# VectorE turns three pairs of head blocks by 32x32 blocks, in place of TensorE transposes

## The chip, the cores and the metric

The kernel runs on one core of one Trainium2 chip. The metric is device time in microseconds (us), the median of a few executions. Names used below: PE is TensorE, PEld its weight loads, DVE is VectorE, ACT is ScalarE, POOL is GpSimd, SP is SyncE, which issues nearly all DMAs.

## The reference

Two layers of a float32 transformer over 256 tokens and a width of 1024. Each layer is a gated feed-forward block, a mixer of three attention branches, and a second feed-forward block. What matters here is the mixer's head work:

```
h = _rmsnorm(x, mix_norm[l])
a_q, a_kv, i_q, i_k, i_w, b_qkv, c_q, c_kv, c_g, m_g = jnp.split(h @ w_in[l], cuts, axis=-1)
i_q = _rope(i_q.reshape(B, T, IDX_HEADS, IDX_DIM), pos)            # 4 index heads of 64
i_k = _rope(i_k[:, :, None, :], pos)[:, :, 0]
y_a = _dsa_attention(a_q, a_k, a_v, i_q, i_k, i_w) @ w_branch_a[l]
b_qkv = b_qkv.reshape(B, T, 3, B_HEADS, HEAD_DIM)                  # 4 heads of 64
y_b = _moba_attention(_rope(b_qkv[:, :, 0], pos), _rope(b_qkv[:, :, 1], pos), b_qkv[:, :, 2]) @ w_branch_b[l]
```

The scores of every branch are products of queries and keys over the 64 columns of a head, and are multiplied by 64 ** -0.5 = 0.125 before the softmax (branches A, B and C; the index scores have a factor of their own).

## The kernel before

**Slabs.** All weights stream through three buffers, slab by slab of 128x2048 values (1 MB, two DMAs of 512 KB). A slab m goes through four hands. SP loads it into `raw` as soon as VectorE has finished slab m-3 (semaphore `lo_done`). ScalarE rounds it into `whi`, once TensorE is done with slab m-3 (`slab_used`). VectorE forms `wlo = raw - whi` (`convert`, L509). TensorE then does three matmuls for each product (L1311 to L1313): with `whi`, with `wlo`, and with the low part of the activations. A full slab is 24 matmuls of 512 columns.

**The projection stage of the mixer.** Slabs 0 to 9 of the mixer are five column groups u = 0 to 4 of `h @ w_in`, two slabs for each. Slabs 10, 11 and 12 are narrow (660, 660 and 440 columns), slab 13 and those behind it are gate weights. When TensorE has done a group, ScalarE copies it out to `proj` (`project_out`, L1153), and VectorE applies the rotation to the heads in it (`rope`, L637 to L643) and leaves the rotated heads in `rs`, which lies in the tile `gates`. `rs` has one block of 128 columns for each two heads: blocks 3 and 4 are the index queries, 6 and 7 branch B's queries, 8 and 9 its keys.

**The order on VectorE** is written out by hand in `mixer`: convert two slabs (m even, m odd), then `rope` of the group whose copy out has just been done, and so on. `rope(l, 1)` stands behind slab 5, `rope(l, 2)` behind slab 7, `rope(l, 3)` behind slab 9, `rope(l, 4)` behind slab 11. Every engine runs its own instructions strictly in that order.

**Fills.** Scores need the heads with the head's columns on partitions, so each block of `rs` is transposed. `FILLS` lists these: TensorE transposes one or two blocks into a PSUM bank (`fill`, L1481; a pair of blocks is four transposes of 128x128), and ScalarE or VectorE copies the bank into `q_t` or `k_t` (`copy_fill`), in turn by the fill's number: even ones ScalarE, odd ones VectorE. The first T1 = 5 fills stand on TensorE between slab 12 and slab 13, the others between slab 13 and slab 14. Fills marked "qs" are scaled by 0.125 on the way.

**Maxima.** For each pair of head groups VectorE adds a mask to the scores and takes row maxima in one operation (`maxima`, L708); the factor -1.0 in it turns the sign, and ScalarE takes the exponential with scale -1.0.

Of the kernel before, what the change touches and what calls it, by code (L numbers as in the profile page):

```python
# [33 lines left out]
P = 128  # L34
SEQ, D, DFF, DEPTH = 256, 1024, 2816, 2
NT = SEQ // P
# [45 lines left out]

FILLS = [((0, 1), "qs", 0), ((2,), "pair", 0), ((3, 4), "q", 2), ((6, 7), "qs", 4), ((8, 9), "k", 2),
         ((14,), "pair", 4), ((15,), "pair", 6), ((10, 11), "qs", 6), ((12, 13), "qs", 8),
         ((16, 17), "n", 0), ((18, 19), "n", 2)]
NFILL = len(FILLS) + 2
T1 = 5

# [23 lines left out]

LAST_ORDER = [0, 2, 1, 3]

V_STEPS = 246
SETUP_WARM, SETUP_G = 1, 19  # L120


def build(nc, x_in, ffn1_w_gate, ffn1_w_up, ffn1_w_down, w_in, cmp_w1_k, cmp_w2_k, cmp_w1_v, cmp_w2_v,
# [3 lines left out]
    with ctx:  # L127
# [229 lines left out]
        def prob_view(b, t):  # L357
            a, w = (0, P) if t == 0 else (512, SEQ)
            return prob[:, b, a:a + 4 * w].rearrange("p (h c) -> p h c", h=4)
# [129 lines left out]
        def _(dve):  # L489
# [156 lines left out]
            def fill_out(l, f):  # L646
# [2 lines left out]
                copy_fill(lambda o, i, k: step(nc.vector.tensor_scalar(o, i, k, None, ALU.mult)), f)  # L649
                at_step["fill", f] = count[0]  # L650

            def cmp_windows(l):

                dve.wait_ge(fill_a, l * 7 + 7)
                own(l)
                for v in range(2):
                    for g in range(2):
                        for a in range(2):
                            win = kvs[:, v, g, 16 * a:16 * a + CMP_STRIDE * NCMP]\
                                .rearrange("p (n j r) -> p j n r", j=8, r=2)[:, :, :, 0]  # L660
                            o = cmpm[:, v, 8 * a:8 * a + 8, g * CPAD:g * CPAD + NCMP]
                            pb = pos_c(l, v)[:, 8 * a:8 * a + 8].unsqueeze(2).broadcast_to([P, 8, NCMP])
                            step(nc.vector.tensor_tensor(o, win, pb, ALU.add), ("windows",))
# [34 lines left out]
            def maxima(l, e):  # L698
                pair, b = PAIRS[e], e % 2
                own(l)  # L700
                dve.wait_ge(sc_ps, l * len(PAIRS) + e + 1)
                if pair != "C":

                    masks = sel_b if pair == "A" else future_b
                    for t in range(NT):
                        mk = masks[:, 0:P] if t == 0 else masks[:, P:3 * P]
                        for h in range(4):
                            step(nc.vector.tensor_tensor_reduce(prob_view(b, t)[:, h, :], score_head(t, h), mk, -1.0,  # L708
                                                                -TAKEN, ALU.add, ALU.min,
                                                                nmax[:, b, 4 * t + h:4 * t + h + 1]), ("max", e, t))  # L710
                if pair == "C":
                    o = prob[:, b, 0:256].rearrange("p (h c) -> p h c", h=16)
                    for t in range(NT):
                        step(nc.vector.tensor_tensor(o[:, 8 * t:8 * t + 8], ps[:, 4, t * P:(t + 1) * P]
                                                     .rearrange("p (h c) -> p h c", h=8),
                                                     kmask_b[:, t, :].unsqueeze(1).broadcast_to([P, 8, CPAD]), ALU.add))
                    own(l)
                    step(nc.vector.tensor_reduce(nmax[:, b, :], o, AX_X, ALU.max, negate=True))
                    own(l)
                    step(nc.vector.tensor_tensor(o, o, nmax[:, b, :].unsqueeze(2).broadcast_to([P, 16, CPAD]),  # L720
                                                 ALU.add), ("max", e, 0))
# [107 lines left out]
            def mixer(l):  # L829
                S = FFN_SLABS  # L830
                prep(l, 1, (2, 3), [2, 3])
                step(nc.vector.memset(cmpm[:, :, :, :], 0.0), ("cmpm zero",))
                last_width = {S + m: nk * LASTU for m, _, nk in M_LAST}
                for m in range(2, 14):
                    convert(l, S + m, last_width.get(S + m, SLAB))
                    if m % 2 and m < 12:
                        rope(l, m // 2 - 1)
                for f in range(1, T1, 2):
                    fill_out(l, f)
                rope(l, 5)  # L840
                convert(l, S + 14)
                dve.wait_ge(cg_done, l + 1)
                step(nc.vector.tensor_scalar(cgt[:, :, :], cgt[:, :, :], 0.5, 0.5, ALU.mult, ALU.add))
                own(l)
                step(nc.vector.tensor_tensor(cgt3[:, :, :, 0], cgt3[:, :, :, 0],
                                             valid[:, :].unsqueeze(2).broadcast_to([P, NT, 8]), ALU.mult))
                for f in range(T1, NFILL, 2):
                    fill_out(l, f)
                cmp_windows(l)
                convert(l, S + 15)  # L850
                hidden_rows(l)
                convert(l, S + 16)
                hidden(l)
                index_scores(l, 0)
                compressed_out(l)
                convert(l, S + 17)
                rounds = [0, 0, 1, 1, 1, 1, 1, 3, 0, 0]
                done = 0
                for e in range(len(SLOTS)):
                    k, before = pair_at(e), pair_at(e - 1)  # L860
                    if e == 1:
                        index_scores(l, 1)
                    if e > 0 and k is not None:
                        maxima(l, k)
                    if e == 4:
                        heads_rest(l, 0)
                    if e == 6:
                        heads_rest(l, 1)


                    late = k in (1, len(PAIRS) - 1)
                    if e > 0 and not late:
                        convert(l, S + 17 + e)
                    if e > 0 and k is not None:
                        scaled(l, k, 0)
                    for _ in range(rounds[e]):
                        select_round(l, done)
                        done += 1
                    if k is not None and k > 1:
                        scaled(l, k, 1)  # L880
                    if late:
                        convert(l, S + 17 + e)
                assert done == 8
                heads_rest(l, 2)
                heads_rest(l, 3)
                convert(l, S + 27)
                for g in range(4):
                    gated(l, 1, g)
                convert(l, S + 28)
                gated(l, 0, 0)  # L890
                gated(l, 0, 1)
                convert(l, S + 29)
                gated(l, 2, 0)
                gated(l, 2, 1)
                gated(l, 0, 2)
                gated(l, 0, 3)
                turned_rest(l, 0)
                turned_rest(l, 1)
                gated(l, 2, 2)
                gated(l, 2, 3)  # L900
                convert(l, S + 30)
                convert(l, S + 31)
                for n in range(2, 4):
                    turned_rest(l, n)
                for m in range(32, 34):
                    convert(l, S + m)
                residual(l, 1, 0, 1.0, S + 32, (4, 5))
# [140 lines left out]
        def _(eng):  # L1048
# [168 lines left out]
            def mixer(l):  # L1217
# [7 lines left out]
                    if m % 2 and m < 12:  # L1225
                        project_out(l, m // 2 - 1)
                project_out(l, 5)
                for f in range(0, NFILL, 2):
                    if f == T1 + 1:
                        convert(l, S + 14)  # L1230
                        eng.wait_ge(proj_done, l * 12 + 12)
                        nc.scalar.activation(cgt[:, :, :], pr[:, :, C_G:C_G + 24], ACT.Tanh,
                                             scale=0.5).then_inc(cg_done, 1)
                    eng.wait_ge(fill_ps, l * NFILL + f + 1)
                    copy_fill(lambda o, i, k: copied.append(nc.scalar.activation(o, i, ACT.Copy, scale=k)), f)
                    copied.pop().then_inc(fill_a, 1)
                    copied.clear()
# [70 lines left out]
        def _(pe):  # L1308
# [152 lines left out]
            def fill(l, f):  # L1461
# [2 lines left out]

                last = next((g for g in range(f - 1, -1, -1) if fill_bank(g) == bank), None)
                if last is not None:
                    if last % 2:
                        wait_step(pe, l, ("fill", last))
                    else:
                        pe.wait_ge(fill_a, l * 7 + last // 2 + 1)  # L1470
                for j in range(len(FILLS[f][0]) if f < len(FILLS) else 1):
                    for t in range(NT):
                        cols_out = slice(j * SEQ + t * P, j * SEQ + (t + 1) * P)
# [137 lines left out]
            def mixer(l):  # L1611
# [34 lines left out]
                    nc.tensor.matmul(ps[:, 7, V_OUT], hid_v[:, :, :].rearrange("p h c -> p (h c)"), w2v(l), start=True,  # L1646
                                     stop=True).then_inc(cmp_ps, 1)

                wait_step(pe, l, ("fill", 9))
                pe.wait_ge(fill_a, l * 7 + 7)  # L1650
                for e in range(len(SLOTS)):
                    k, before = pair_at(e), pair_at(e - 1)
                    if e == 1:
# [191 lines left out]
```

## Time and profile before

| what | value |
|---|---|
| median of 3 runs | 1169.6 us (1169.31 to 1169.7) |
| the profiled execution | 1169.55 us, span 1167.8 us |
| PE busy | 1159.0 us, 99% |
| PEld busy | 948.0 us, 81% |
| DVE busy | 914.3 us, 78% |
| ACT busy | 584.1 us, 50% |
| POOL busy | 32.2 us, 3% |
| mean granted clock of PE | 0.998 |
| read from HBM | 209.28 MB, 180 GB/s over the span |

The span runs from the first to the last recorded instruction; the execution's own time is 1.75 us longer. Matmuls overlap: one of 512 columns lasts 0.39 us in the record, and the next starts 0.227 us after it. So 24 of them, one slab, take 5.44 us. Layer 0's mixer has its projection stage from about 191 to 260 us, layer 1's from about 768 to 838 us.

### The profile page before, as it was taken

The page shows a single profiled execution, that of the slowest core. Times are in us where ns is not written, and L with a number is a line of the kernel's source. Part 1 is how long each engine was busy: PE and PEld are TensorE (multiplying, and loading weights), DVE is VectorE, ACT ScalarE, POOL GpSimd, SP SyncE. Part 2 cuts the span into 40 slices and gives each one's busy share as a digit, 9 for nine tenths or more (in the row PEclk, how much of TensorE's full clock was granted, in tenths as well). Part 3 has the DMA queues.
Part 4 walks back from the last instruction along what each step waited for, and adds up shares of the span by engine and source line. Part 5 has one row for each costly group of instructions (what it writes and reads, how often), then busy time and mean ns, then how long its engine had stood idle before and what let it go on. Part 6 is the DMA issues. An engine that isn't in the chain of part 4 may idle for free.

```text
span 1167.8 us, 16506 instructions
## 1 busy us (share of the span) xinstructions
PE 1159.0 (99%) x5605; PEld 948.0 (81%) x5605; DVE 914.3 (78%) x1662; ACT 584.1 (50%) x759; POOL 32.2 (3%) x67
## 2 busy tenths in 40 slices
PE   9999999999999999999999999999999999999997
PEld 7888888887777888888888888888877788888886
DVE  6877786769977688778788887777798695988775
ACT  6443445447774454344454444454578635444433
POOL 2000000001000000000000000000010000000000
PEclk9999999999999999999999999999999999999999
DMA  8566554755425546655546556646653344655560
GB/s 285 194 207 216 183 196 157 236 192 162 140 76 180 180 146 214 216 191 181 198 169 209 182 169 211 216 156 182 200 179 109 140 138 157 228 187 172 202 233 36
DMA packets 148993, 210.99 MB, mean 181 GB/s; under 512 B 8161, under 2 KB 109137, under 8 KB 148945
## 3 DMA queue, kind: packets, MB, share of 16 engines
q1 hardware_dynamic: 148256, 209.64, 53.5%
q10 hardware_dynamic: 688, 0.71, 0.2%
q8 instruction: 29, 0.48, 0.2%
q14 instruction: 20, 0.16, 0.0%
HBM read 209.28 MB, written 1.05 MB: 180 GB/s over the span
## 4 chain that ended last, share of the span: by engine, by line
PE 95%; DVE 1%; ACT 1%; issue 1%; DMA 0%; POOLq 0%; POOL 0%; DVEq 0%
PE ps L1311 29%; PE ps L1313 29%; PE ps L1312 29%; PE ps L1520 2%; PE ps L1548 2%; PE ps L1576 1%; PE ps L1361 1%; PE ps L1330 1%; PE ps L1481 1%; DVE scr L571 1%; ACT whi L1058 1%; PE ps L1493 0%; ACT p_t L1071 0%; PE ps L1607 0%; PE ps L1567 0%
## 5 line engine op out<-in xcount | busy, mean ns | idle before, releaser
L1058 ACT ACTIVATE whi<-raw 128x2048 fp32r<-128x2048 f32 (+1 forms) x195 | 365.7, 1879 | 277.8 <-PE ps L1313 276.2
L509 DVE TENSOR_TENSOR wlo<-raw,whi 128x2048 fp32r<-128x2048 f32 (+1 forms) x195 | 433.6, 2243 | 78.3 <-ACT whi L1058 51.1
L1311 PE MATMUL ps<-whi,ht_hi 128*128 128x512 f32 (+1 forms) x1192 | 466.9, 392 | 0.0
L1313 PE MATMUL ps<-whi,ht_lo 128*128 128x512 f32 (+1 forms) x1192 | 461.1, 387 | 0.0
L1312 PE MATMUL ps<-wlo,ht_hi 128*128 128x512 f32 (+1 forms) x1192 | 460.6, 386 | 0.0
L1313 PEld LDWEIGHTS ps<-whi,ht_lo 128*128 128x128 f32 x1192 | 223.9, 188 | 45.9
L1311 PEld LDWEIGHTS ps<-whi,ht_hi 128*128 128x128 f32 x1192 | 224.0, 188 | 44.3 <-issue 0.8
L1312 PEld LDWEIGHTS ps<-wlo,ht_hi 128*128 128x128 f32 x1192 | 224.2, 188 | 43.5
L571 DVE STREAM_TRANSPOSE scr<-scr 32x128 f32<-32x128 f32 x624 | 188.9, 303 | 9.3
L1311 PE MATMUL ps<-whi,at_hi 128*128 128x512 f32 x336 | 131.7, 392 | 1.0 <-DVE at_lo L577 1.0
L1312 PE MATMUL ps<-wlo,at_hi 128*128 128x512 f32 x336 | 130.9, 389 | 0.0
L1313 PE MATMUL ps<-whi,at_lo 128*128 128x512 f32 x336 | 130.8, 389 | 0.0
L1099 ACT ACTIVATE scr<-ps,rstd 128x256 f32<-128x256 f32 x88 | 36.9, 470 | 134.7 <-PE ps L1313 133.2
L561 DVE SCALAR_TENSOR_TENSOR scr<-ps,rstd,scr 128x256 f32<-128x256 f32 x88 | 38.5, 479 | 63.0 <-ACT scr L1099 63.0
L1311 PEld LDWEIGHTS ps<-whi,at_hi 128*128 128x128 f32 x336 | 63.1, 188 | 15.6 <-DVE at_lo L577 1.9
L1313 PEld LDWEIGHTS ps<-whi,at_lo 128*128 128x128 f32 x336 | 63.1, 188 | 13.2
L1312 PEld LDWEIGHTS ps<-wlo,at_hi 128*128 128x128 f32 x336 | 63.1, 188 | 12.9
L1187 ACT ACTIVATE prob<-prob,nmax 128x128 f32<-128x128 f32 (+1 forms) x96 | 42.4, 445 | 6.4 <-DVE nmax L708 6.4
L1086 ACT ACTIVATE ht_hi<-ps,cols 128x256 fp32r<-128x256 f32 x47 | 19.2, 472 | 29.9 <-PE ps L1330 29.9
L1107 ACT ACTIVATE at_hi<-scr 128x512 fp32r<-128x512 f32 x39 | 24.0, 615 | 16.8 <-DVE scr L571 16.7
L1153 ACT ACTIVATE proj<-ps,rstd 128x512 f32<-128x512 f32 (+1 forms) x24 | 14.2, 645 | 35.7 <-PE ps L1313 35.7
L1200 ACT ACTIVATE p_t<-ps 128x512 f32<-128x512 f32 x36 | 20.9, 591 | 19.3 <-PE ps L1548 19.1
(172 smaller groups left out, 691.2 us busy)
## 6 DMA issues: line engine op xcount, KB each, us to landing
raw<-in_ffn_w_down_dram SPq DMA_DIRECT2D x88, 512.0 KB, 4.6
raw<-in_w_in_dram SPq DMA_DIRECT2D x88, 512.0 KB, 4.5
raw<-in_ffn_w_gate_dram SPq DMA_DIRECT2D x85, 512.0 KB, 3.7
raw<-in_ffn_w_up_dram SPq DMA_DIRECT2D x85, 512.0 KB, 4.7
raw<-in_w_out_dram SPq DMA_DIRECT2D x16, 512.0 KB, 4.5
raw<-in_w_branch_c_dram SPq DMA_DIRECT2D x8, 512.0 KB, 4.1
raw<-in_w_branch_b_dram SPq DMA_DIRECT2D x4, 512.0 KB, 3.9
raw<-in_w_branch_a_dram SPq DMA_DIRECT2D x4, 512.0 KB, 4.1
```

Source lines behind the costliest of these rows:

```text
L509: nc.vector.tensor_tensor(wlo[:, n, 0:w], raw[:, n, 0:w], whi[:, n, 0:w].bitcast(F32), ALU.subtract).then_inc(lo_done, 1)
L561: nc.vector.scalar_tensor_tensor(act[:, t, :], ps[:, bank, FSTEP:2 * FSTEP], rstd[:, t:t + 1], sg[:, t, :], ALU.mult, ALU.mult).then_inc(a ...
L571: ins = nc.vector.transpose(dst[q:q + 32, :, :, a:a + 32], src[a:a + 32, :, :, q:q + 32])
L1058: nc.scalar.activation(whi[:, n, 0:w], raw[:, n, 0:w], ACT.Copy).then_inc(hi_done, 1)
L1099: nc.scalar.activation(sg[:, t, :], ps[:, t + (first_bank(f) if first else 0), 0:FSTEP], ACT.Silu, scale=rstd[:, t:t + 1]).then_inc(silu_d ...
L1107: nc.scalar.activation(act_parts(i)[0], turned_product(l, f, i), ACT.Copy).then_inc(ath, 1)
L1187: ins = nc.scalar.activation(pv, pv, ACT.Exp, scale=-1.0, bias=nmax[:, b, 4 * t + h:4 * t + h + 1], accum_out=den[:, b, 4 * t + h:4 * t + ...
L1311: nc.tensor.matmul(o, xh, wh, start=start, stop=False)
L1312: nc.tensor.matmul(o, xh, wl, start=False, stop=False)
L1313: return nc.tensor.matmul(o, xl, wh, start=False, stop=stop)
L1520: ins = nc.tensor.matmul(score_head(t, h), q_t[row, qb + h // 2, t * P:(t + 1) * P], k_t[row, kb + kstep * (h // 2), 0:nk], start=opens, s ...
L1548: ins = nc.tensor.transpose(ps[:, pt_bank(e, f), h * P:(h + 1) * P], prob_view(b, t)[:, h, kt * P:(kt + 1) * P], ident[:, :])
```

## The change

The index queries, branch B's queries and branch B's keys leave `FILLS`. VectorE turns each of these pairs of blocks itself, from `rs` straight into `q_t` or `k_t`: 16 instructions for each pair, one for each pair of 32-row and 32-column strips, of 32x128 values. They stand in VectorE's order behind `rope(l, 1)` (index queries, "I"), behind `rope(l, 2)` (B's keys, "K"), and behind the convert of slab 9 (B's queries, "B"). Since B's queries are no longer scaled on a copy, the factor in B's masking operation becomes -0.125. The engine for each remaining fill is given by `by_act`.

```diff
-FILLS = [((0, 1), "qs", 0), ((2,), "pair", 0), ((3, 4), "q", 2), ((6, 7), "qs", 4), ((8, 9), "k", 2),
-         ((14,), "pair", 4), ((15,), "pair", 6), ((10, 11), "qs", 6), ((12, 13), "qs", 8),
-         ((16, 17), "n", 0), ((18, 19), "n", 2)]
+FILLS = [((0, 1), "qs", 0), ((2,), "pair", 0), ((14,), "pair", 4), ((15,), "pair", 6),
+         ((10, 11), "qs", 6), ((12, 13), "qs", 8), ((16, 17), "n", 0), ((18, 19), "n", 2)]
 NFILL = len(FILLS) + 2
-T1 = 5
+T1 = 2
+
+DVE_TURNS = {"I": (3, "q", 2), "K": (8, "k", 2), "B": (6, "q", 4)}
+
+def by_act(f):
+    return f % 2 == 0 if f < T1 else (f - T1) % 2 == 1
...
+            def turn_blocks(l, name):
+
+                b, kind, b0 = DVE_TURNS[name]
+                into = (q_t if kind == "q" else k_t)[:, b0:b0 + 2, :].rearrange("p b (t c) -> p t b c", t=NT)
+                own(l)
+                for a in range(0, P, 32):
+                    for q in range(0, P, 32):
+                        step(nc.vector.transpose(into[q:q + 32, :, :, a:a + 32], rs[a:a + 32, :, b:b + 2, q:q + 32]))
...
+                    sign = -ATT_SCALE if pair == "B" else -1.0
...
-                            step(nc.vector.tensor_tensor_reduce(prob_view(b, t)[:, h, :], score_head(t, h), mk, -1.0,
+                            step(nc.vector.tensor_tensor_reduce(prob_view(b, t)[:, h, :], score_head(t, h), mk, sign,
...
                 for m in range(2, 14):
                     convert(l, S + m, last_width.get(S + m, SLAB))
+                    if m == 9:
+                        turn_blocks(l, "B")
                     if m % 2 and m < 12:
                         rope(l, m // 2 - 1)
-                for f in range(1, T1, 2):
-                    fill_out(l, f)
+                    if m == 5:
+                        turn_blocks(l, "I")
+                    if m == 7:
+                        turn_blocks(l, "K")
+                for f in range(T1):
+                    if not by_act(f):
+                        fill_out(l, f)
```

Here is VectorE's order in layer 0 from the end of `rope(l, 1)` to slab 10. In the kernel before (L643 is the last step of a `rope`, L509 a convert):

```order
L643 TENSOR_TENSOR gates<-gates,prob 128x2x256
L509 TENSOR_TENSOR wlo<-raw,whi 128x2048 x2
L637 TENSOR_TENSOR gates<-proj,cos_s 128x2x256
L638 TENSOR_TENSOR prob<-proj,sin_s 128x2x4x32
L640 TENSOR_TENSOR prob<-proj,sin_s 128x2x4x32
L643 TENSOR_TENSOR gates<-gates,prob 128x2x256
L509 TENSOR_TENSOR wlo<-raw,whi 128x2048 x2
L637 TENSOR_TENSOR gates<-proj,cos_s 128x2x512
L638 TENSOR_TENSOR prob<-proj,sin_s 128x16x32
L640 TENSOR_TENSOR prob<-proj,sin_s 128x16x32
L643 TENSOR_TENSOR gates<-gates,prob 128x2x512
L509 TENSOR_TENSOR wlo<-raw,whi 128x660 x2
```

The same place in the changed kernel (L652 is the last step of a `rope`, L518 a convert, L668 the new transposes):

```order
L652 TENSOR_TENSOR gates<-gates,prob 128x2x256
L668 STREAM_TRANSPOSE q_t<-gates 32x2x2x32 x16
L518 TENSOR_TENSOR wlo<-raw,whi 128x2048 x2
L646 TENSOR_TENSOR gates<-proj,cos_s 128x2x256
L647 TENSOR_TENSOR prob<-proj,sin_s 128x2x4x32
L649 TENSOR_TENSOR prob<-proj,sin_s 128x2x4x32
L652 TENSOR_TENSOR gates<-gates,prob 128x2x256
L668 STREAM_TRANSPOSE k_t<-gates 32x2x2x32 x16
L518 TENSOR_TENSOR wlo<-raw,whi 128x2048 x2
L668 STREAM_TRANSPOSE q_t<-gates 32x2x2x32 x16
L646 TENSOR_TENSOR gates<-proj,cos_s 128x2x512
```

Three rows of 16 have come in: ahead of the converts of slabs 6 and 7, ahead of those of slabs 8 and 9, and ahead of `rope(l, 3)`, which the converts of slabs 10 and 11 stand behind.

TensorE's order in layer 0 around the first fills, between slab 12 (220 columns wide) and slab 13. Before:

```order
L1313 MATMUL ps<-whi,ht_lo 128x220
L1311 MATMUL ps<-whi,ht_hi 128x220
L1312 MATMUL ps<-wlo,ht_hi 128x220
L1313 MATMUL ps<-whi,ht_lo 128x220
L1481 MATMUL ps<-ident,gates 128x128 x18
L1311 MATMUL ps<-whi,ht_hi 128x512
```

And now:

```order
L1341 MATMUL ps<-whi,ht_lo 128x220
L1339 MATMUL ps<-whi,ht_hi 128x220
L1340 MATMUL ps<-wlo,ht_hi 128x220
L1341 MATMUL ps<-whi,ht_lo 128x220
L1509 MATMUL ps<-ident,gates 128x128 x6
L1339 MATMUL ps<-whi,ht_hi 128x512
```

Twelve of the eighteen transposes are gone there; the 24 behind slab 13 stay as they were.

## Rows read from the trace of the kernel before

**Rows 1.** The page: busy time by engine, and the chain that ended last.

```profile
PE 1159.0 (99%) x5605; PEld 948.0 (81%) x5605; DVE 914.3 (78%) x1662; ACT 584.1 (50%) x759; POOL 32.2 (3%) x67
...
PE 95%; DVE 1%; ACT 1%; issue 1%; DMA 0%; POOLq 0%; POOL 0%; DVEq 0%
```

**Rows 2.** PE's waits on a product: total us, times, longest us.

```profile
PE ps L1311 <- DVE at_lo L577: 1.0, 2, 0.5
```

**Rows 3.** Timeline of PE, first fills and slab 13: start, us, instruction.

```profile
250.60 2.17 PE L1481 MATMUL ps<-ident,gates 128*128 128x128 f32 x18
252.53 0.48 PE L1311 MATMUL ps<-whi,ht_hi 128*128 128x512 f32 x1
```

**Rows 4.** Timeline of DVE, feed-forward: 16 transposes, then two converts.

```profile
113.87 5.05 DVE L571 STREAM_TRANSPOSE scr<-scr 32x128 f32<-32x128 f32 x16
118.95 4.49 DVE L509 TENSOR_TENSOR wlo<-raw,whi 128x2048 fp32r<-128x2048 f32 x2
```

**Rows 5.** Timeline of DVE, projection stage, layer 0; [idle before <-releaser].

```profile
214.10 0.69 DVE L637 TENSOR_TENSOR gates<-proj,cos_s 128x512 f32<-128x512 f32 x1 [2.38 <-ACT proj L1153]
...
218.55 0.69 DVE L643 TENSOR_TENSOR gates<-gates,prob 128x512 f32<-128x512 f32 x1
219.16 4.49 DVE L509 TENSOR_TENSOR wlo<-raw,whi 128x2048 fp32r<-128x2048 f32 x2
224.98 0.69 DVE L637 TENSOR_TENSOR gates<-proj,cos_s 128x512 f32<-128x512 f32 x1 [1.34 <-ACT proj L1153]
...
226.99 2.28 DVE L509 TENSOR_TENSOR wlo<-raw,whi 128x2048 fp32r<-128x2048 f32 x1
231.19 2.29 DVE L509 TENSOR_TENSOR wlo<-raw,whi 128x2048 fp32r<-128x2048 f32 x1 [1.91 <-ACT whi L1058]
235.86 1.23 DVE L637 TENSOR_TENSOR gates<-proj,cos_s 128x1024 f32<-128x1024 f32 x1 [2.38 <-ACT proj L1153]
...
239.47 0.84 DVE L509 TENSOR_TENSOR wlo<-raw,whi 128x660 fp32r<-128x660 f32 x1
...
249.51 2.29 DVE L509 TENSOR_TENSOR wlo<-raw,whi 128x2048 fp32r<-128x2048 f32 x1 [0.96 <-issue]
```

**Rows 6.** Timeline of PE: the first matmul of slabs 6, 8 and 10.

```profile
223.48 0.39 PE L1311 MATMUL ps<-whi,ht_hi 128*128 128x512 f32 x1
...
234.36 0.39 PE L1311 MATMUL ps<-whi,ht_hi 128*128 128x512 f32 x1
...
245.24 0.26 PE L1311 MATMUL ps<-whi,ht_hi 128*128 128x220 f32 x1
```

**Rows 7.** Timeline of PE, then of DVE: a restart behind a DVE result.

```profile
425.78 0.50 PE L1311 MATMUL ps<-whi,at_hi 128*128 128x512 f32 x1 [0.52 <-DVE at_lo L577]
426.12 0.40 PE L1312 MATMUL ps<-wlo,at_hi 128*128 128x512 f32 x1
...
425.04 0.69 DVE L577 TENSOR_TENSOR at_lo<-scr,at_hi 128x512 fp32r<-128x512 f32 x1
```

**Rows 8.** SP's issue of slab 13's two DMAs, and their landing.

```profile
240.34 0.89 SPq L1722 DMA_DIRECT2D raw<-in_w_in_dram  x2
...
DMA to landing us min/median/max: 3.7/4.2/4.6
```

**Rows 9.** Timeline of ACT: its part of slab 13.

```profile
247.50 1.92 ACT L1058 ACTIVATE whi<-raw 128x2048 fp32r<-128x2048 f32 x1 [0.33 <-PE ps L1313]
```

**Rows 10.** Timeline of DVE, layer 1: the converts of slabs 6 and 7.

```profile
796.36 4.48 DVE L509 TENSOR_TENSOR wlo<-raw,whi 128x2048 fp32r<-128x2048 f32 x2
```

**Rows 11.** Timeline of DVE: two ops of 128 values in a row.

```profile
285.62 0.28 DVE L708 CUSTOM_DVE_ANT_0 prob<-ps,future_b 128x128 f32<-128x128 f32 x1
...
285.83 0.29 DVE L708 CUSTOM_DVE_ANT_0 prob<-ps,future_b 128x128 f32<-128x128 f32 x1
```

**Rows 12.** Windows of PE at the end: length, busy (x), granted clock, DMA.

```profile
1161.50:1162.00 0.50, 0.00 (x0) 1.00 0.00 0
...
1163.50:1164.00 0.50, 0.00 (x0) 0.54 0.00 0
```

More of the change, by code:

```diff
@@ L80 @@
 }
-FILLS = [((0, 1), "qs", 0), ((2,), "pair", 0), ((3, 4), "q", 2), ((6, 7), "qs", 4), ((8, 9), "k", 2),
-         ((14,), "pair", 4), ((15,), "pair", 6), ((10, 11), "qs", 6), ((12, 13), "qs", 8),
-         ((16, 17), "n", 0), ((18, 19), "n", 2)]
+FILLS = [((0, 1), "qs", 0), ((2,), "pair", 0), ((14,), "pair", 4), ((15,), "pair", 6),
+         ((10, 11), "qs", 6), ((12, 13), "qs", 8), ((16, 17), "n", 0), ((18, 19), "n", 2)]
 NFILL = len(FILLS) + 2
-T1 = 5
+T1 = 2
+DVE_TURNS = {"I": (3, "q", 2), "K": (8, "k", 2), "B": (6, "q", 4)}
+def by_act(f):
+    return f % 2 == 0 if f < T1 else (f - T1) % 2 == 1
+NACT = sum(by_act(f) for f in range(NFILL))
 SCORE_ORDER = [(1, 0), (0, 1), (3, 0), (2, 1), (1, 1), (0, 0), (3, 1), (2, 0)]
@@ L117 @@
 LAST_ORDER = [0, 2, 1, 3]
-V_STEPS = 246
+V_STEPS = 293
 SETUP_WARM, SETUP_G = 1, 19
@@ L650, in fill_out @@
                 at_step["fill", f] = count[0]
+            def turn_blocks(l, name):
[5 more added lines that the diff above has]
+                        step(nc.vector.transpose(into[q:q + 32, :, :, a:a + 32], rs[a:a + 32, :, b:b + 2, q:q + 32]))
             def cmp_windows(l):
-                dve.wait_ge(fill_a, l * 7 + 7)
+                dve.wait_ge(fill_a, (l + 1) * NACT)
                 own(l)
@@ L846, in mixer @@
                                              valid[:, :].unsqueeze(2).broadcast_to([P, NT, 8]), ALU.mult))
-                for f in range(T1, NFILL, 2):
-                    fill_out(l, f)
+                for f in range(T1, NFILL):
+                    if not by_act(f):
+                        fill_out(l, f)
                 cmp_windows(l)
@@ L1227, in mixer @@
                 project_out(l, 5)
-                for f in range(0, NFILL, 2):
+                for f in [f for f in range(NFILL) if by_act(f)]:
                     if f == T1 + 1:
@@ L1466, in fill @@
                 if last is not None:
-                    if last % 2:
+                    if by_act(last):
+                        pe.wait_ge(fill_a, l * NACT + sum(by_act(g) for g in range(last + 1)))
+                    else:
                         wait_step(pe, l, ("fill", last))
-                    else:
-                        pe.wait_ge(fill_a, l * 7 + last // 2 + 1)
                 for j in range(len(FILLS[f][0]) if f < len(FILLS) else 1):
@@ L1647, in compressed @@
                                      stop=True).then_inc(cmp_ps, 1)
-                wait_step(pe, l, ("fill", 9))
-                pe.wait_ge(fill_a, l * 7 + 7)
+                wait_step(pe, l, ("fill", T1 + 4))
+                pe.wait_ge(fill_a, (l + 1) * NACT)
                 for e in range(len(SLOTS)):
```

## The prediction

> **What bounds the kernel now.** I read the page first: PE is busy 99% of the span and is 95% of the chain that ended last [rows 1]. So a microsecond taken from PE counts in full, and so does a microsecond that PE is made to wait. Then the waits of PE: on a product of the main path it waited twice in all, 1.0 us [rows 2]. There is no idle time in PE that a new wait could hide in. VectorE is busy 78% of the span [rows 1]; whether it has room is a question of the place, so I read its timeline through the projection stage, row by row, beside the times at which PE starts each slab.
>
> There the reader is to see three idle gaps on VectorE between the end of `rope(l, 1)` and slab 10: 1.34, 1.91 and 2.38 us, together 5.63 us [rows 5]. And a lead: how long before PE's start of a slab its `wlo` is finished. The convert pair of slabs 6 and 7 starts at 219.16 [rows 5]; one convert lasts 2.29 us, so slab 6 is ready at 221.45, and PE starts it at 223.48 [rows 6]: a lead of 2.0 us. Slab 10 is ready at 239.47 + 0.84 = 240.31 and starts at 245.24 [rows 5, 6]: 4.9 us. Layer 1 shows the same pair at 796.36 [rows 10], 577.2 us later with nearly the same length, so I work out layer 0 and double it.
>
> **What is removed.** Three fills, twelve transposes of PE in each layer. Eighteen take from 250.60 to 252.53 [rows 3], 0.107 us each, so twelve are 1.29 us, 2.6 us for both layers. Two copies of ScalarE and one of VectorE go too; neither engine is waited for there, so I count them as nothing. Even if all of it counted, 2.6 us is 0.22% of 1169.6, and 0.2% (2.3 us) is about what a measurement of this kernel can tell from no change.
>
> Not all of it counts. Slab 13 is converted from 249.51 to 251.80 [rows 5], and PE starts it at 252.53 behind eighteen transposes [rows 3]. A restart behind a VectorE result costs PE 0.05 us from the end of the result (425.73) to the matmul (425.78), and that matmul keeps the next away for 0.34 us where it is otherwise 0.227 [rows 7]: 0.16 us together. So slab 13 can't start before 251.96, only 0.57 us earlier, whatever becomes of the transposes.
>
> **What is added.** Each turn is 16 transposes of 32x128 values, the form that the feed-forward stage already runs: 16 of them last 5.05 us, and the next convert starts 0.03 us later [rows 4]. The tiles and strides differ, and each now signals a semaphore; I keep 5.05 us. A turn behind a `rope` also waits for its last result: that ends at 218.55 + 0.69 = 219.24, against 219.16 for an unwaiting successor [rows 5], so 0.12 us with the wait's own 0.04. Turns I and K push their successors back by 5.20 us each. Turn B has waited already and pushes by 5.08. In each layer that is 15.48 us of VectorE.
>
> The three are queued ahead of converts, and every convert has PE waiting behind it. Step by step, layer 0:
>
> Turn I ends at 224.33, slab 6 is converted from 224.36 to 226.65, and PE starts it at 226.81, not 223.48: **3.33 us late**. Slab 7 is ready at 228.85, ahead of PE.
>
> `rope(l, 2)` follows at once, at 228.78 (its input is long there), and takes 2.09 us as in [rows 5] (224.98 to 226.99, and 0.08 to its end). Turn K runs 230.91 to 235.96, slab 8 is ready at 238.28, PE starts it at 238.44. Without this wait it would have been 234.36 + 3.33 = 237.69 [rows 6]: **0.75 us more**.
>
> Slab 9 is ready at 240.49, in time. Turn B runs 240.41 to 245.46, `rope(l, 3)` takes the 3.61 us from 235.86 to 239.47 [rows 5], and slab 10 is ready at 249.94. PE starts it at 250.10; 245.24 + 4.08 would be 249.32: **0.78 us more**, 4.86 in all. The balance says the same: 15.48 added, less 5.63 of idle gaps now filled, is 9.85 later for slab 10's convert; taking off the lead of 4.93, itself less the 0.16 of the restart, leaves 5.08, near the 4.86 of the steps, whose converts overlap by 0.08 at each joint.
>
> **What is late next** is a load. SP loads slab 13 when VectorE has finished slab 10: it issues at 240.34, right behind 240.31. The second of its two DMAs is issued some 0.43 us later and lands 4.6 us after that, so 5.0 us in all [rows 5, 8]. Before, the data were there at 245.4 and ScalarE began at 247.50, when PE had finished slab 10 [rows 9], so the load was hidden by 2.1 us. Now the issue is at 249.97, the data come at 255.0, and PE has been done with slab 10 since 252.3. ScalarE takes 1.92 us [rows 9], VectorE follows 0.09 us later (249.42 to 249.51) and takes 2.29, and PE starts slab 13 at 255.0 + 1.92 + 0.09 + 2.29 + 0.16 = 259.46, not 252.53: **6.93 us late**. The transposes that PE no longer runs there are swallowed in that wait. Behind it I find nothing late: `rope(l, 5)`, slab 14's convert and the second fills keep ahead of a PE that is 6.9 us later.
>
> **The factor in B's mask** is an immediate of the same 32 operations: nothing. The new order of the remaining fills leaves ScalarE and VectorE the same ones as before behind slab 13.
>
> **The sum.** 2 x 6.93 = 13.9 us on the profiled execution's 1169.55 (span 1167.8 and 1.75 around it; it stands within 0.05 us of the median): **1183.4 us**, 1.2% slower.
>
> **Bounds.** The price of a transpose is the term that counts. The cheapest row for 128 values on VectorE is a masking operation whose successor starts 0.21 us later [rows 11], 3.4 us for a turn; the dearest is the 5.05. The same steps with 3.4 give no wait at slabs 8 and 10 and slab 13 at 254.5, 2.0 us late: 1173.5. At 6 us for a turn each step is dearer by the difference, 2.9 us per layer: 1189. I take 5.05, since it is the same instruction on the same shape. For the load: if it were hidden, slab 13 would start 4.3 us late, and the time be 1178.1.
>
> The Trainium skill ("VectorE: DVE Perf Modes", The three transpose paths) lists a 128x128 bf16 transpose at 390 ns on TensorE and 311 ns on VectorE, which makes VectorE look the cheaper place. By it, as an estimate, a turn (four such squares) would be 1.2 us. The trace disagrees for float32 strips: 5.05 us for the same four squares, and 0.107 us of PE's time for each of its own [rows 3, 4].
>
> **Rivals.**
>
> *The turns are hidden (not slower).* If turn I took no more than about 1.7 us (219.28 + 1.7 + 0.03 + 2.29 + 0.16 = 223.46), slab 6 would be in time, the others would vanish in the gaps, and slab 13 would start 0.57 us earlier in each layer: 1168.4 us. What speaks for it is only that another form of operation is cheap; against it 16 x 0.316 us in [rows 4]. It is also what the price that the skill lists would give. Chance 0.04, with 0.01 of it for a gain over 0.2%.
>
> *Cheaper transposes, half hidden:* 1170 to 1177, centre 1173.5. Chance 0.08.
>
> *The chain of VectorE without the load:* 1177 to 1181, centre 1178.1, if the load's landing shortens on an otherwise idle queue or SP is not held. For it: 4.6 us was measured with slab 14's load close behind. Chance 0.14.
>
> *The granted clock falls in the new gaps.* PE would stand idle about 3 us twice in each layer: from 223.65 to 226.7 and before slab 13. At the end of the kernel PE is idle from 1161.50 at a granted 1.00 (2.4 GHz), and 2 us later the clock is at 0.54, on its way to 0.50 (1.2 GHz) [rows 12]. So both gaps are long enough to be suspect. After the first, up to 1.5 us of slower work would vanish in the waits at slabs 8 and 10; after the second all of it counts. If the clock stayed low for a third to two thirds of a slab of 5.44 us, PE would lose half of that, 0.9 to 1.8 us in each layer, to be added: 1185.2 to 1187.0; for a low clock over a whole slab's matmuls, 5.4 us in each, 1194. Chance 0.20 for 1185 to 1189. The skill ("TensorE: Matmul & The Clock Gate", Why this matters for your kernels) names idle gaps between bursts of matmuls as a cause of throughput drops; no row of before shows such a gap inside the work, so whether these count is open.
>
> *Dearer still,* above 1189 (slower strips, or a longer low clock): 0.06.
>
> **How the numbers follow.** The forecast itself, 1181 to 1185, has 0.48. With the load hidden (0.14) and the clock (0.20) the range 1177 to 1189 holds 0.82. Slower by over 0.2% has all but the first rival and the near edge of the second: 0.95; within 0.2% 0.04; faster 0.01.
>
> **What would show it.** PE in layer 0: slab 6 starts near 226.8 behind a VectorE `wlo`, slab 8 near 238.4, slab 10 near 250.1, slab 13 near 259.5. PE's waits name DVE's convert (the line of L509) with about 8 us in each layer, where there was none. VectorE has no gap from `rope(l, 1)` to slab 10. ScalarE's part of slab 13 waits for a DMA. Six transposes in place of eighteen. The prediction is wrong if a turn is far from 5.05 us, if slab 13's data come earlier than 5 us after slab 10's convert, if PEclk drops, or if a later wait gives time back.

## The result, and the profile after

The changed kernel takes 1190.51 us (median of 4, 1189.39 to 1191.3) against 1169.45 us (1169.04 to 1169.7): ratio 1.0178, 95% interval 1.0167 to 1.0190. It is 21.1 us slower; 13.9 were forecast, and 1190.5 lies above the range of 1177 to 1189. The rows shown are of one execution of 1191.3 us, span 1189.5.

The page of the changed kernel, the lines that answer to [rows 1]:

```profile
PE 1164.7 (98%) x5581; PEld 950.7 (80%) x5581; DVE 941.6 (79%) x1756; ACT 581.7 (49%) x755; POOL 32.2 (3%) x67
...
PE 88%; DVE 6%; ACT 2%; issue 2%; DMA 1%; SPq 0%; POOLq 0%; POOL 0%; DVEq 0%; ACTq 0%
```

PE's share of the chain went from 95% to 88%; VectorE and a DMA are on it now. PE's busy time is higher by 5.7 us although it runs 24 transposes fewer: a first hint that it worked at a slower pace somewhere. The waits of the changed kernel (total us, times, longest):

```profile
PE ps L1339 <- DVE wlo L518: 15.5, 6, 4.7
...
ACT whi L1086 <- DMA raw<-in_w_in_dram: 8.8, 2, 5.4
```

Six waits of PE on a convert, three in each layer, where [rows 2] had none. The timeline of PE at the six, layer 0 and then layer 1 (the reader should look at the brackets: idle before, and who ended it):

```profile
228.46 0.53 PE L1339 MATMUL ps<-whi,ht_hi 128*128 128x512 f32 x1 [3.41 <-DVE wlo L518]
252.70 0.34 PE L1339 MATMUL ps<-whi,ht_hi 128*128 128x220 f32 x1 [0.62 <-DVE wlo L518]
263.63 0.77 PE L1339 MATMUL ps<-whi,ht_hi 128*128 128x512 f32 x1 [4.68 <-DVE wlo L518]
...
818.16 0.47 PE L1339 MATMUL ps<-whi,ht_hi 128*128 128x512 f32 x1 [3.41 <-DVE wlo L518]
842.02 0.34 PE L1339 MATMUL ps<-whi,ht_hi 128*128 128x220 f32 x1 [0.20 <-DVE wlo L518]
851.45 0.47 PE L1339 MATMUL ps<-whi,ht_hi 128*128 128x512 f32 x1 [3.19 <-DVE wlo L518]
```

These are slabs 6, 10 and 13. VectorE's timeline through layer 0's stage, to be laid beside [rows 5]:

```profile
215.51 0.69 DVE L646 TENSOR_TENSOR gates<-proj,cos_s 128x512 f32<-128x512 f32 x1 [2.38 <-ACT proj L1181]
...
220.67 5.32 DVE L668 STREAM_TRANSPOSE q_t<-gates 32x128 f32<-32x128 f32 x16
226.02 4.49 DVE L518 TENSOR_TENSOR wlo<-raw,whi 128x2048 fp32r<-128x2048 f32 x2
...
232.55 5.32 DVE L668 STREAM_TRANSPOSE k_t<-gates 32x128 f32<-32x128 f32 x16
237.90 4.49 DVE L518 TENSOR_TENSOR wlo<-raw,whi 128x2048 fp32r<-128x2048 f32 x2
242.31 5.30 DVE L668 STREAM_TRANSPOSE q_t<-gates 32x128 f32<-32x128 f32 x16
248.11 1.23 DVE L646 TENSOR_TENSOR gates<-proj,cos_s 128x1024 f32<-128x1024 f32 x1 [0.50 <-DVE q_t L668]
...
251.72 1.59 DVE L518 TENSOR_TENSOR wlo<-raw,whi 128x660 fp32r<-128x660 f32 x2
...
261.19 2.29 DVE L518 TENSOR_TENSOR wlo<-raw,whi 128x2048 fp32r<-128x2048 f32 x1 [5.96 <-ACT whi L1086]
```

The first row stands 1.41 us later than its fellow in [rows 5], ahead of anything that the change touches. That comes from the kernel's start in this execution (in a second profile of the same kernel, below, that point is within 0.1 us of before, and in the other runs' profiles it lies between 213.1 and 214.9), so 1.41 is taken off all differences in layer 0. The three gaps of 1.34, 1.91 and 2.38 us are gone, as forecast; each turn is 5.3 us, not 5.05; and in layer 0 a gap of 0.50 us, which I had not foreseen, follows turn B. In layer 1 the successor starts 0.10 us behind the turn's end, and so has no bracket:

```profile
832.01 5.31 DVE L668 STREAM_TRANSPOSE q_t<-gates 32x128 f32<-32x128 f32 x16
837.43 1.23 DVE L646 TENSOR_TENSOR gates<-proj,cos_s 128x1024 f32<-128x1024 f32 x1
```

ScalarE's part of slab 13 in both layers:

```profile
259.19 1.91 ACT L1086 ACTIVATE whi<-raw 128x2048 fp32r<-128x2048 f32 x1 [5.35 <-DMA raw<-in_w_in_dram]
...
847.01 1.91 ACT L1086 ACTIVATE whi<-raw 128x2048 fp32r<-128x2048 f32 x1 [3.42 <-DMA raw<-in_w_in_dram]
```

It waits for the load now. SP issued it at 252.58 and 841.90, so the data took 6.6 us in layer 0 and 5.1 in layer 1. The windows of PE (length, busy, granted clock, DMA share, GB/s) behind the first gap and behind the third:

```profile
227.00:228.00 1.00, 0.00 (x0) 1.00 0.00 0
228.00:229.00 1.00, 0.54 (x2) 0.87 0.00 0
229.00:230.00 1.00, 1.00 (x3) 0.50 0.61 72
231.00:232.00 1.00, 1.00 (x4) 0.50 1.04 393
232.00:233.00 1.00, 1.00 (x5) 0.93 1.04 377
...
262.00:263.00 1.00, 0.00 (x0) 0.93 0.33 119
263.00:264.00 1.00, 0.37 (x1) 0.50 0.06 25
264.00:269.00 5.00, 5.00 (x13) 0.50 0.64 210
269.00:270.00 1.00, 1.00 (x5) 0.65 0.29 35
270.00:272.00 2.00, 2.00 (x10) 1.00 0.89 281
```

The clock is at 0.50 (1.2 GHz) from about 228.7 to 232.1 and from 262.9 to 269.7. In layer 1 it falls behind slab 6 as well (819.2 to 822.7), but not behind slab 13's gap of 3.19 us. In the low stretch matmuls start 0.427 us apart, not 0.227.

What the execution's own marks add up to: slab 13 starts at 263.63, before at 252.53, so 9.7 us late in layer 0 with the 1.41 taken off. The second fills show what the low clock added:

```profile
272.00 1.47 PE L1509 MATMUL ps<-ident,gates 128*128 128x128 f32 x12
...
857.02 1.47 PE L1509 MATMUL ps<-ident,gates 128*128 128x128 f32 x12
```

The row stood at 258.08 before (and 577.2 later in layer 1). Layer 0 is late by 13.9 - 1.4 = 12.5, of which 2.8 came between slab 13's start and here; layer 1 adds 7.8, all of it in place when slab 13 starts. With the 1.4 of the start that is 21.7, the whole difference of the two profiled executions (1191.3 - 1169.55).

### The profile page after: what moved, and what is told of

It is laid out like the page before. It is cut to its first block, busy times and chain, and to the rows that moved or that the text cites. A ratio compares the mean times of both kernels' runs of the same rounds, so it can differ in the third digit from the quotient of the medians.

```text
span 1189.5 us, 16548 instructions
## 1 busy us (share of the span) xinstructions
PE 1164.7 (98%) x5581; PEld 950.7 (80%) x5581; DVE 941.6 (79%) x1756; ACT 581.7 (49%) x755; POOL 32.2 (3%) x67
## 4 chain that ended last, share of the span: by engine, by line
PE 88%; DVE 6%; ACT 2%; issue 2%; DMA 1%; SPq 0%; POOLq 0%; POOL 0%; DVEq 0%; ACTq 0%
PE ps L1339 27%; PE ps L1341 26%; PE ps L1340 26%; DVE wlo L518 2%; PE ps L1548 2%; DVE q_t L668 2%; PE ps L1389 1%; PE ps L1576 1%; PE ps L1604 1%; ACT whi L1086 1%; DMA raw<-in_w_in_dram 1%; PE ps L1358 1%; DVE scr L580 1%; DVE gates L646 0%; PE ps L1509 0%
## 5 line engine op out<-in xcount | busy, mean ns | idle before, releaser
L518 DVE TENSOR_TENSOR wlo<-raw,whi 128x2048 fp32r<-128x2048 f32 (+1 forms) x195 | 433.3, 2243 | 81.5 <-ACT whi L1086 51.6
L542 DVE SCALAR_TENSOR_TENSOR ht_lo<-ps,cols,ht_hi 128x256 fp32r<-128x256 f32 x48 | 20.7, 477 | 13.1 <-ACT ht_hi L1114 13.1
```

Of the source, the lines that this page charges most:

```text
L518: nc.vector.tensor_tensor(wlo[:, n, 0:w], raw[:, n, 0:w], whi[:, n, 0:w].bitcast(F32), ALU.subtract).then_inc(lo_done, 1)
```

## The experiments

Before's median was 1169.25 to 1169.48 us in all of them. Times are medians; the interval is that of the ratio to before.

**The changed kernel again.** No edit.

> The changed kernel once more, unchanged, on the chip of the others of this call, so that its times and its clock can be set beside theirs. Expected: 1188.5 to 1191.5 us, the runs further apart than those of before (0.7 us), since whether the clock falls behind slab 13's gap differs from one execution to the next.

Measured: 1189.77 us (1188.63 to 1191.26), ratio 1.0172 (1.0156 to 1.0187). The runs are 2.6 us apart. In its profile VectorE's stage begins with before's, so the 1.41 above is no effect of the change. Here the clock falls behind all four long gaps, the one ahead of slab 13 in layer 1 too:

```profile
849.75 0.47 PE L1339 MATMUL ps<-whi,ht_hi 128*128 128x512 f32 x1 [3.29 <-DVE wlo L518]
```

```profile
848.00:851.00 3.00, 1.25 (x6) 1.00 0.77 247
851.00:852.00 1.00, 1.00 (x4) 0.56 0.72 209
852.00:854.00 2.00, 2.00 (x6) 0.50 1.01 392
```

From slab 13's start to the second fills PE takes 8.06 us in layer 0 (262.11 to 270.17) and 7.20 in layer 1 (849.75 to 856.95), where it took 5.55 before: the low clock costs 2.5 and 1.6 us behind slab 13 in this execution, and cost 2.8 and nothing in the first. Slab 13's load took 6.6 and 5.2 us. The changed kernel is told below as 1189.8 to 1190.5.

**TensorE kept at work in the gaps.**

```diff
+            def spare_matmuls(n):
+                for _ in range(n):
+                    nc.tensor.matmul(ps[:, 7, :], ht_hi[:, 0, 0:P], ht_hi[:, 0:2, :].rearrange("p k c -> p (k c)"),
+                                     start=True, stop=True)
...
+                        if (u, a) == (3, 0):
+                            spare_matmuls(12)
...
                     fill(l, f)
+                spare_matmuls(14)
```

> The changed kernel with spare matmuls of TensorE into an unread PSUM bank, 12 ahead of slab 6 and 14 behind the first fills (0.23 us each, so 2.7 and 3.2 us), which fill most of the gaps in which TensorE waits. The output is the reference's. Theory (the low clock behind the gaps is part of the loss): the granted clock stays at 1.00 in the projection stages, and the time falls by the 2.8 us that the low clock cost behind slab 13's gap in layer 0, and by nothing for the falls behind slab 6, which the waits at slabs 8 and 10 swallow: 1186 to 1189 us. Rival (the clock behind the gaps costs nothing that counts): 1190 to 1191. Rival (all of what went beyond my forecast is the clock): 1183 to 1185.

Measured: 1185.69 us (1185.34 to 1185.85), ratio 1.0137 (1.0120 to 1.0153), 4.1 to 4.8 us less than the changed kernel, by doing more work on the engine that bounds it. The theory's range was missed by 0.3 us on the low side. The windows of this run stay at full clock:

```profile
225.00:235.00 10.00, 9.31 (x41) 1.00 0.76 220
250.00:265.00 15.00, 13.65 (x87) 1.00 0.80 278
```

But the clock isn't all that differs. Layer 0's load for slab 13, issued at 251.15, brought its data 5.25 us later, not 6.6:

```profile
256.40 1.92 ACT L1086 ACTIVATE whi<-raw 128x2048 fp32r<-128x2048 f32 x1 [4.57 <-DMA raw<-in_w_in_dram]
```

So some 1.4 of the 4.1 to 4.8 us are the load's, and the rest is near what the low clock took in the profiles of the changed kernel, 2.8 and 4.2 us. That the spare matmuls made the load quicker isn't shown. The runs are 0.5 us apart where the changed kernel's are 1.9 to 2.6; that fits a clock that falls in some executions only, but the load varies as well.

**The same behind the first fills alone.** Only the 14 spare matmuls.

> The changed kernel with the 14 spare matmuls behind the first fills alone, and none ahead of slab 6, so that the granted clock may fall behind slab 6 and not behind slab 13's gap. Theory (what a low clock takes behind slab 6 is swallowed by the waits at slabs 8 and 10): the same as with both sets, 1185 to 1187 us. Rival (the fall behind slab 6 costs its 1.8 to 2.8 us in each layer): 1189 us and more.

Measured: 1186.28 us (1185.37 to 1186.67), ratio 1.0144 (1.0127 to 1.0161). Its clock does fall behind slab 6:

```profile
225.00:235.00 10.00, 8.95 (x32) 0.83 0.87 248
```

and the time is within 0.6 us of the run with both sets. Slab 10 starts 6.0 us late in layer 0 of both profiles (250.28 and 251.27, less 245.24, and the stage begins 1.0 us earlier here than before). So what a fall behind slab 6 takes is gone by slab 10, while waits at slabs 8 and 10 follow, as forecast, and the low clock is paid for behind slab 13's gap. The load took 6.4 us in layer 0 here, 1.2 more than with both sets, and PE waited for slab 13 again, behind the spare matmuls:

```profile
261.03 0.47 PE L1339 MATMUL ps<-whi,ht_hi 128*128 128x512 f32 x1 [1.28 <-DVE wlo L518]
```

**The twelve transposes given back to TensorE**, into banks that nobody reads.

```diff
+                for n, b in enumerate((3, 4, 6, 7, 8, 9)):
+                    for t in range(NT):
+                        nc.tensor.transpose(ps[:, 6 + n % 2, t * P:(t + 1) * P], rs[:, t, b, :], ident[:, :])
                 wide(l, S + 13, 0, 4, (0, 1), 512, 0, KD - 1)
```

> The changed kernel, but TensorE still does the twelve transposes that the change took from it, into banks that nobody reads. Theory (slab 13's wait swallows them): no change that can be measured against the changed kernel, 1189 to 1191 us; if the shorter gap keeps the clock up now and then, 1 to 2 us less. Rival (what TensorE is spared counts in full): 2.6 us more, 1193.

Measured: 1188.91 us (1186.49 to 1189.76), ratio 1.0158 (1.0141 to 1.0174), no slower than without them. PE still waits behind them, 1.2 us less than in the changed kernel:

```profile
261.71 0.77 PE L1339 MATMUL ps<-whi,ht_hi 128*128 128x512 f32 x1 [3.52 <-DVE wlo L518]
```

In layer 1 the wait is 1.92 us, and the clock falls even so:

```profile
848.29 0.47 PE L1339 MATMUL ps<-whi,ht_hi 128*128 128x512 f32 x1 [1.92 <-DVE wlo L518]
```

```profile
849.00:852.00 3.00, 3.00 (x9) 0.50 0.91 292
```

What the change saves TensorE is worth nothing at the place where it is saved.

**One semaphore signal for a turn**, not sixteen.

```diff
-                        step(nc.vector.transpose(into[q:q + 32, :, :, a:a + 32], rs[a:a + 32, :, b:b + 2, q:q + 32]))
+                        ins = nc.vector.transpose(into[q:q + 32, :, :, a:a + 32], rs[a:a + 32, :, b:b + 2, q:q + 32])
+                step(ins)
```

> The changed kernel with one semaphore signal at the end of each turn of 16 transposes, in place of sixteen. Theory A (the signals make a turn 5.32 us long where the feed-forward's takes 5.05): turns of 5.05 us, and 3 x 0.27 = 0.8 us less in each layer, some 1189 us. Theory B (the tiles and strides do it): turns stay at 5.32 and the time at 1190 to 1191.

Measured: 1188.94 us (1187.09 to 1190.44), ratio 1.0169 (1.0152 to 1.0186). The turn itself, in VectorE's timeline:

```profile
219.10 5.05 DVE L668 STREAM_TRANSPOSE q_t<-gates 32x128 f32<-32x128 f32 x16
224.18 4.49 DVE L518 TENSOR_TENSOR wlo<-raw,whi 128x2048 fp32r<-128x2048 f32 x2
```

Theory A holds: 5.05 us again, so fifteen signals cost 0.27 us, and tiles and strides cost nothing. The time's fall of 0.8 to 1.6 us fits but lies within the runs' spread.

**Turn B behind slab 11's convert.**

```diff
-                    if m == 9:
+                    if m == 11:
                         turn_blocks(l, "B")
```

> The changed kernel with turn B moved from ahead of rope 3 to behind the convert of slab 11, where VectorE had a gap of 5.0 us. The same instructions, another place. Theory (the place decides: converts are held up, and slab 13's load hangs on slab 10's convert): no wait at slab 10, slab 13's load is hidden again, slab 13 starts some 3.8 to 4.3 us late in each layer: 1177 to 1180 us. Rival (VectorE's added work decides wherever it stands): no change, 1189 to 1191. Rival (only the wait at slab 10 goes, the load stays late): 1186 to 1188.

Measured: 1179.19 us (1178.51 to 1179.84), ratio 1.0079 (1.0063 to 1.0096), as the theory said. The same instructions at another place are worth 11 us. ScalarE no longer waits for a load in this stage, and PE waits four times, 7.9 us in all:

```profile
PE ps L1339 <- DVE wlo L518: 7.9, 4, 3.4
```

**Slab 10's convert ahead of rope 3.** All turns stay.

```diff
+                    if m == 10:
+                        rope(l, 3)
-                    if m % 2 and m < 12:
+                    if m % 2 and m < 12 and m != 9:
                         rope(l, m // 2 - 1)
```

> The changed kernel with one convert moved: slab 10's stands ahead of rope 3 (3.6 us) instead of behind it; nothing else moves, and all turns stay where they are. Theory (slab 13's load hangs on slab 10's convert and is a term of its own): the convert ends 3.6 us earlier, near 247.5 us, TensorE doesn't wait for it, the data of slab 13 come near 253, ScalarE waits under 2 us for them and not 3.4 to 5.5, and each layer is 2.5 to 4 us shorter: 1181.5 to 1185 us. Rival (VectorE's chain alone counts, the load was never a limit): the next converts are as late as they were, 1189 to 1190.

Measured: 1179.36 us (1178.37 to 1180.08), ratio 1.0083 (1.0066 to 1.0099). Right in kind, but 2 us better than the best that was expected. VectorE finishes slab 10 at 247.20, and ScalarE takes slab 13 as soon as PE lets it, not when a DMA does:

```profile
246.35 0.85 DVE L518 TENSOR_TENSOR wlo<-raw,whi 128x660 fp32r<-128x660 f32 x1
...
254.08 1.92 ACT L1088 ACTIVATE whi<-raw 128x2048 fp32r<-128x2048 f32 x1 [0.33 <-PE ps L1343]
```

I had expected a wait of up to 2 us to be left. None is, and with a gap of 0.54 us ahead of slab 13 the clock doesn't fall there. Behind slab 6 it still falls in both layers, as with turn B moved (0.50 from 226.3 to 233.1 and from 810.0 to 813.4 here), and with no wait behind to swallow it that is part of the 10 us that are left. So one convert of 0.8 us, held up by a rotation of 3.6, was worth about 10 us: the wait at slab 10, the load's and the clock's.

**Turn I alone.** Branch B's blocks are fills again, unscaled.

```diff
-FILLS = [((0, 1), "qs", 0), ((2,), "pair", 0), ((14,), "pair", 4), ((15,), "pair", 6),
+FILLS = [((0, 1), "qs", 0), ((2,), "pair", 0), ((6, 7), "q", 4), ((8, 9), "k", 2), ((14,), "pair", 4), ((15,), "pair", 6),
...
-T1 = 2
+T1 = 4
```

with the calls of turns K and B left out.

> Turn I alone; branch B's queries and keys go back to TensorE's fills (unscaled, the factor stays in the mask). Theory (the wait at slab 6 alone, and a clock that is low behind it, which no later wait swallows now): slab 6 starts 3.6 us late, the granted clock falls behind it and costs 1.8 to 2.8 us more, four transposes fewer give back 0.4: 5.0 to 6.0 us in each layer, 1179.5 to 1181.5 us. Rival (the fall is harmless here too): 3.2 us in each layer, 1175.9. Rival (a third of the added VectorE work, a third of the loss): 1176.5.

Measured: 1178.99 us (1177.47 to 1180.90), ratio 1.0088 (1.0073 to 1.0103), 0.5 us under the theory's range and 2.5 to 3.1 above the rivals. The profile tells why runs can lie apart: the same gap of 3.4 us ahead of slab 6 in both layers, a low clock behind the first only. (Of the 3.4 us between the runs, 2.4 are between their spans, 1175.5 to 1177.9; the rest lies outside the span and is not explained.)

```profile
225.00:235.00 10.00, 8.30 (x30) 0.83 0.79 229
...
805.00:820.00 15.00, 11.59 (x52) 1.00 0.76 216
```

Layer 0 is 4.8 us late at the second fills, layer 1 adds 3.1: a fall costs 1.7 us when no later wait swallows it, and a gap of this length doesn't bring it each time.

**The factor alone**, in the kernel before.

```diff
-((6, 7), "qs", 4)
+((6, 7), "q", 4)
...
+                    sign = -ATT_SCALE if pair == "B" else -1.0
```

> The kernel before with nothing but the factor 0.125 moved from the copy of branch B's queries to B's masking operation. Theory: the same time, within 0.1%. Rival (the factor in the masking operation costs something): 32 operations, over 0.2% only if each took 70 ns more.

Measured: 1169.61 us, 11 runs, ratio 1.0003 (0.9994 to 1.0012). Nothing.

**Two turns where VectorE has room.** B's queries behind slab 8's convert, the index queries behind slab 11's, one signal each; B's keys stay a fill.

```diff
...
-                    if m == 9:
+                    if m == 8:
                         turn_blocks(l, "B")
+                    if m == 11:
+                        turn_blocks(l, "I")
...
-                    if m == 5:
-                        turn_blocks(l, "I")
-                    if m == 7:
-                        turn_blocks(l, "K")
```

> Only two turns, with one semaphore signal each, where VectorE has room: branch B's queries behind the convert of slab 8, the index queries behind the convert of slab 11; B's keys stay a fill of TensorE. Theory (a turn costs nothing where converts and slab 13's load keep their lead, and TensorE is spared eight transposes, of which 0.4 to 0.57 us per layer count): no wait of TensorE on a convert over 0.5 us, clock 1.00, 1168.3 to 1169.0 us against 1169.5, a gain too small to be told with certainty. Rival (every turn on VectorE costs what it lasts): 1169.5 + 4 x 5.05 = 1190, or half of it, 1180.

Measured: 1168.66 us, 11 runs, ratio 0.9994 (0.9985 to 1.0003). The same time as before, with 20 us of transposes (4 x 5.05) on VectorE. The turns in its timeline, and all its waits on a convert:

```profile
229.07 5.05 DVE L668 STREAM_TRANSPOSE q_t<-gates 32x128 f32<-32x128 f32 x16
...
241.55 5.04 DVE L668 STREAM_TRANSPOSE q_t<-gates 32x128 f32<-32x128 f32 x16
...
PE ps L1338 <- DVE wlo L518: 0.5, 1, 0.5
```

It is the best version here, and no gain that can be told from none.

## Why the prediction was wrong

The sign and the path were right: converts held up behind the turns, and a load behind the last of them. Three terms of the sum were mis-sized, and one, which stood among the rivals, belonged in it. The time came out where only "dearer still" had put it, at a chance of 0.06, and by both of the causes named there, slower strips and a longer low clock, with the load beside them.

**The clock.** The step that failed first is the sum's silence on it: "The granted clock falls in the new gaps" had a chance of 0.20 and no place in the 1183.4. It happened, and took 2.8 us behind slab 13 in the first profile (layer 0 alone) and 4.2 in the second (2.5 and 1.6). Its price there was 1.8 to 3.6 us for both layers, because I let the low stretch last a third to two thirds of a slab. Behind the gap of 4.68 us it lasted 6.8 us, 6.1 of them after PE had resumed. That a fall behind slab 6 would vanish in later waits was right.

**The load.** That slab 13's load becomes the last thing to end was right: ScalarE's rows name it, and they no longer do when turn B or slab 10's convert is moved, each of which frees 10 to 11 us. Its 5.0 us from issue to data were 5.1 to 5.2 in layer 1 but 6.6 in layer 0, in both profiles of the changed kernel: 1.7 us in all. Why is open. The converts of slabs 10 and 11 run together now, so the next load is issued under a us later, where before there were 1.4 us between them. But layer 1 has the same spacing, and so have two other runs whose layer 0 took 5.25 us (both sets of spare matmuls) and 5.3 (one signal), so the spacing alone doesn't make it.

**The turn.** "I keep 5.05 us" was 0.27 too low, three times in each layer: 1.6 us of VectorE's time in all. The semaphore signals named in that sentence are the cause, shown by the run with one signal.

**The wait behind turn B.** "Turn B has waited already and pushes by 5.08" looked ahead of the turn and not behind it: `rope(l, 3)` waits for the turn's last result. It starts 0.50 us after the turn's recorded end in layer 0 and 0.10 in layer 1, where a wait on a rotation's result costs 0.04. That is 0.5 us for both layers; why layer 0 has more is open. With the turns this puts slab 10's start 6.05 us late in layer 0 (252.70 less 245.24 and 1.41) and 5.65 in layer 1 (842.02 less 822.45 and layer 0's 13.92), where the steps had 4.86. Slab 10's first matmul in layer 1 of the kernel before:

```profile
822.45 0.26 PE L1311 MATMUL ps<-whi,ht_hi 128*128 128x220 f32 x1
```

Together, by the rows of the two profiles of the changed kernel: 13.9 as forecast, 1.2 and 0.8 for the turns and the wait (layers 0 and 1), 1.7 for the load, and 2.8 or 4.2 for the clock. That is 20.4 us in the first, whose difference without the late start was 20.3, and 21.8 in the second (1191.26 less 1169.55, and a start 0.1 earlier). The medians, 21.1 and 20.5 us slower, lie about there.

**Step by step.** Slab 6 was forecast 3.33 us late and is 3.57 (228.46 less 223.48 and 1.41). Slab 8 was to wait 0.75 us more and doesn't in these rows: the low clock had made PE late already; with the clock held up it waits 0.71. Slab 13: 6.93 forecast, 9.7 in layer 0 and 7.8 in layer 1. The 2.6 us saved on TensorE are swallowed, as said. The factor costs nothing, as said. Behind slab 13 no other wait came up, as said. The rival by which the turns hide had its deciding point at 1.7 us for a turn; here it was 5.3. By the price for a 128x128 square in the Trainium skill ("VectorE: DVE Perf Modes", The three transpose paths) a turn would have been 1.2 us, as an estimate (four squares of 311 ns); the float32 strips measured four times that.

## What to carry to other kernels

Work moved off the bounding engine is paid at the first thing queued behind it on the other one: find each convert, copy or load behind it, and compare its lead with what is put ahead. A total such as "78% busy" says nothing of it; three turns cost 21 or 10 us by their place, and two of them, well placed, nothing. Then follow a late step to the load that it frees. When a sum leaves the matmul engine idle for some 2 to 5 us, as here, put the low clock into the sum, not among the rivals. And read each term at its own rows: the difference of two runs, 4.1 to 4.8 us with the spare matmuls, held a quicker load beside the clock.

## What the runs showed of the hardware

- In the profiles of the changed kernel and of its variants, PE has 24 gaps of 1.9 to 4.7 us in the projection stages, and the granted clock fell to 0.50 in or behind 22 of them. It did not behind 3.19 us (the changed kernel, layer 1) and 3.41 us (turn I alone, layer 1); the shortest gap with a fall was 1.92 us, behind eighteen transposes. Gaps of 0.54 to 1.28 us did not bring it. The fall came 2.0 to 4.7 us after PE had stopped, in some cases when it was at work again; in [rows 12] it came 2 us after PE's last matmul. In the changed kernel's layer 0 the clock came back 3.7 us after PE had resumed at slab 6 and 6.1 us after it had at slab 13. What it took, where nothing swallowed it, was 1.6 to 3.0 us for a fall. The Trainium skill ("TensorE: Matmul & The Clock Gate", Why this matters for your kernels) names such gaps as a cause of throughput drops, and the runs agree.
- Sixteen transposes of 32x128 float32 values last 5.05 us with one semaphore signal and 5.32 with sixteen. The Trainium skill ("VectorE: DVE Perf Modes", The DRAIN you can't avoid) says of copies that a signal after each costs nothing; here each costs 18 ns.
- A rotation that waits for a turn's last transpose starts 0.10 us after its recorded end in layer 1 of every profile, and in layer 0 too where turn B or I stands behind slab 11. In layer 0 of the changed kernel's order it is 0.50 us, in six profiles; what adds the 0.4 is open. Behind a float32 multiply or add such a wait costs 0.04.
- The data of one load of 1 MB (slab 13, layer 0) came 6.4 to 6.8 us after its issue in four profiles and 5.25 and 5.3 us after it in two. No run shows what decides it.
